# RWKV recurrence on one core: the state chain of a tile set among the doubling levels of the next tile, gate products in five blocks

## Chip, cores and metric

The kernel runs on one core of a Trainium2 chip. The metric is the device time of one launch, in microseconds (us), as the median over runs.

## What is computed

One step of a hybrid streaming encoder layer: a combined input projection of RMSNorm(h), chunked band attention for half of the heads, an RWKV-7 recurrence for the other half, gates, and an output projection. The change touches the recurrence. Per head it is

```
def step(S, inp):
    r_t, w_t, k_t, v_t, kk_t, a_t = inp
    sa = jnp.einsum('bhij,bhj->bhi', S, -kk_t)
    S = (S * w_t[:, :, None, :] + sa[..., None] * (kk_t * a_t)[:, :, None, :]
         + v_t[..., None] * k_t[:, :, None, :])
    y = jnp.einsum('bhij,bhj->bhi', S, r_t)
    return S, y
```

followed by a group norm of y, the bonus `sum(r * k * r_k) * v` and the gate silu(g). There are 2048 prompt frames (16 tiles of 128) and 8 running streams of 16 frames, which form a seventeenth tile with states of their own.

## The kernel before

Everything is in float32, or in two float32r parts for the wide products. The kernel has four phases: projection with attention, the shifted projections, `rwkv_phase` (recurrence, with the gate projection inside it), and the output projection.

In `rwkv_phase` a tile has two chunks of 64 frames and eight heads in four pairs, so eight units. A float32 product of 64x64 is recorded as two matmul entries, and the two halves of a unit run beside each other. For a tile t, in the order of its data:

- `mix`: LoRA products, sigmoids (`sig`, `a_gate` on ScalarE), the scan `acc` on VectorE, and the norm of the keys: `kk`, `kk_sq` on GpSimd, `kk_hi` on ScalarE, `kk_lo` on VectorE, and the `kk_sum` product on TensorE.
- `front`: `g_run`, `inv_g` (ScalarE, after a table load), `kk_n`, `ahat`, `rhat`, `bt`, `kt` (VectorE), `kmod`, `rkr`, `bmul` (GpSimd); the bonus products, the turns (`turn_two`), and the four Gram matrices B0, K0, B1, K1, masked by VectorE (L2123); then `a_eye` (GpSimd L1749), `z2`, `y2` (VectorE L2129, L2132) and the crossed copy (ScalarE L1910).
- levels (in `back`): the inverse of a triangular 64x64 matrix of each unit by doubling in five levels (three in the last tile). A level is the W products (L2401), the mask `w_mat` (VectorE L2145), the Q products (L2413), ScalarE's copy of the result (L1918, L1921) and VectorE's two transposes (L2150, L2153). W of the next level needs the copy, Q of the next level needs the transposes.
- chain (in `back`): for chunk 0 and then chunk 1: products of the state (L2422) into rhs, ScalarE's copy (L1930), `solve` (L2442), ScalarE's copy of u (L1934), products to the state (L2506), VectorE's add and decay (L2160, L2136), and `read_out` (L2451) into y.
- `tail`: `y_sum`, `y_centred`, `y_var` on VectorE, `y_sq` and the root on ScalarE, and on GpSimd `v_bonus` (L1784), then scale, gain, base and sum (L1787 to L1799).
- `gates`: 48 wide products (128x128 by 128x512) in two halves j of 24 for the gate projection, with splits of the input into two parts.

The order of each engine's queue is written by hand. Every run is a generator that yields a key ahead of each step, and `merged` always takes the step with the lowest key of the runs of a round; where keys are equal, the earlier run goes first. Engines meet by semaphores alone, so a key sets only an order. In round t the runs are `back(t)`, `tail(t-1)`, `front(t+1)`, `mix(t+2)` and `gates(t+1)`:

```
                run = [back(t, u, mode_of(t))]
                if t > 0:
                    run.append(tail(t - 1, 1 - u, "p"))
```

The levels stand at keys 4.1 l and 4.1 l + 2.1 for W and Q of level l, the chain at 20.5 and 26.85, the Grams at 25.05 and 28.15. Between W and Q, and between Q and W, stands a gate block (`GATE_BLOCKS`) of 4 or 5 products each: ten blocks a round, the last of 8. `free_bank` gives out two PSUM banks in turn in the order of `JOB_ORDER`; u is written into the level bank.

Of the kernel before, what the change touches and what calls it, by code (L numbers as in the profile page):

```python
# [22 lines left out]
P = 128  # L23
# [1213 lines left out]
def rwkv_phase(nc, io, shared):  # L1237

    with ExitStack() as ctx:
# [51 lines left out]
        bonus = sb2("bonus", [P, UNITS])  # L1291
# [42 lines left out]
        ps_u, ps_streams = ps_level[:, 0:512], ps_level[:, 512:1024]  # L1334
# [56 lines left out]
        def cols_of(n):  # L1391
# [8 lines left out]
        JOBS = ("decay", "iclr", "kk_sum", "k_tok", "b_tok", "B0", "B1", "K0", "K1", "bonus")  # L1400
# [9 lines left out]
        rhs_written, rhs_ready, u_written, u_ready = sem("rhs_written"), sem("rhs_ready"), sem("u_written"), sem("u_ready")  # L1410
# [5 lines left out]
        dec_keys = sem("dec_keys")  # L1416
# [3 lines left out]
        JOB_ORDER = ((("bonus", -1), ("decay", 0), ("k_tok", -1), ("B0", -1), ("B1", -1)),  # L1420
                     (("iclr", 0), ("b_tok", -1), ("K0", -1), ("K1", -1), ("kk_sum", 0)))
# [11 lines left out]
        def job_before(t, name):  # L1433
            b, i, off = place(name)
            r = t - off
            while r >= 0:
# [4 lines left out]
                if 0 <= r + o <= DEC:  # L1441
                    return n, r + o
            return None

        def free_bank(t, name):
# [4 lines left out]
            return ps_job[place(name)[0]], job_written[name]  # L1450

# [16 lines left out]
        def past(eng, t, *names):  # L1468

            for n in names:  # L1470
# [3 lines left out]
                       [(6, 12), (7, 13), (8, 22), (9, 26.1), (10, 28.4), (11, 28.5)])  # L1474
        GATE_BLOCKS = (((1.1, 5), (3.2, 5), (5.2, 5), (7.3, 5), (9.3, 4)), ((13.4, 4), (17.5, 4), (19.6, 4), (23.6, 4), (28.9, 8)))
        FIRST_SPLITS = (4, 5), (6, 7)
        GATE_W_AT = ((13, 14), (14, 15), (15, 18), (18.5, 23.5))
# [28 lines left out]
        def tiles(eng, front, back, mix=nothing, tail=nothing, gates=nothing, first_gates=nothing, out=nothing):  # L1506
# [44 lines left out]
        def _(sp):  # L1551
# [20 lines left out]
            def first_gates(t, u, mode):  # L1572
                if t == 1:
# [5 lines left out]
                    yield 30  # L1579
# [19 lines left out]
            def gates(t, u, mode):  # L1599
                if t == DEC:  # L1600
# [4 lines left out]
                    yield 11.8  # L1605
# [5 lines left out]
                for j in range(2):  # L1611
                    if t == DEC and j == 1:
                        yield 16
# [7 lines left out]
                        yield 30  # L1621
# [3 lines left out]
                    if j == 0 and t < DEC:  # L1625
# [3 lines left out]
                        yield 24.6  # L1629
                        sp.wait_ge(u_ready, 2 * t - 1)  # L1630
                    else:
                        yield (13.2, 33.5)[j]
# [20 lines left out]
            def mix(t, u, mode):  # L1653
# [7 lines left out]
                yield 24.7  # L1661
# [1364 lines left out]
```

## Time and profile before

| | us |
|---|---|
| median of 3 runs | 1640.91 (1640.88 to 1646.04) |
| the profiled execution | span 1640.3; no other time of it is recorded |
| TensorE busy | 1591.8 (97%) |
| VectorE, ScalarE, GpSimd busy | 806.8, 879.3, 498.8 |
| DMA | 184.4 MB, 112 GB/s on average |

Span is the time from the first to the last instruction. Busy TensorE counts an entry from its start to the end of its pipeline, so overlapping and waiting entries look alike, and starts say more than busy time. The recurrence phase lies between about 850 and 1440 us; a round begins with the W products of level 0.

### The profile page before, as it was taken

The numbers are of one execution on the slowest core, as the hardware profiler recorded it, in microseconds if no ns is written. First come the engines' busy times: TensorE is split into PE (matmuls) and PEld (weight loads), VectorE is DVE, ScalarE is ACT, GpSimd is POOL, SyncE is SP. The second block draws the span as 40 slices with busy tenths as digits, with TensorE's granted clock in tenths as the row PEclk, the third lists the DMA queues.
The fourth block names the chain that finished last, engine by engine and source line by source line (L and its number), as shares of the span: only waits on it lengthen the run. The fifth ranks groups of instructions, "written<-read, shape, count | busy, mean of one in ns | idle before, by whom it ended". The sixth has DMA issues, their size and how long they took to land. (4 is left out here: it accounts for less than half of the span.)

```text
span 1640.3 us, 46809 instructions
## 1 busy us (share of the span) xinstructions
PE 1591.8 (97%) x20218; PEld 1301.9 (79%) x20218; DVE 806.8 (49%) x1153; ACT 879.3 (54%) x1833; POOL 498.8 (30%) x354
## 2 busy tenths in 40 slices
PE   8999999999999899999998999999999997999999
PEld 7788888888888788899986777777777876777787
DVE  4344544454445531121226677667677677544432
ACT  6466566656665631222237777777777776224320
POOL 1423221222121012221223456455556456400000
PEclk9999999999999999999999999999999999999999
DMA  6323211122113543433353232232232236286652
GB/s 244 88 82 94 70 51 61 55 73 61 60 43 116 196 134 123 135 105 106 114 174 125 70 93 79 73 93 69 83 87 89 81 97 206 70 318 225 206 173 77
DMA packets 136302, 184.43 MB, mean 112 GB/s; under 512 B 59153, under 2 KB 88337, under 8 KB 135842
## 3 DMA queue, kind: packets, MB, share of 16 engines
q1 hardware_dynamic: 129186, 170.83, 32.3%
q10 hardware_dynamic: 6912, 10.62, 1.8%
q8 instruction: 160, 2.62, 0.7%
q14 instruction: 44, 0.36, 0.1%
HBM read 122.42 MB, written 59.55 MB: 111 GB/s over the span
## 5 line engine op out<-in xcount | busy, mean ns | idle before, releaser
L681 PE MATMUL a_ps_proj<-a_w_hi,a_x_hi 128*128 128x512 f32 x384 | 157.6, 410 | 2.5 <-ACT a_qk L431 1.4
L681 PE MATMUL a_ps_proj<-a_w_hi,a_x_lo 128*128 128x512 f32 x384 | 151.6, 395 | 0.0
L681 PE MATMUL a_ps_proj<-a_w_lo,a_x_hi 128*128 128x512 f32 x384 | 151.1, 393 | 0.0
L584 DVE SCALAR_TENSOR_TENSOR a_stage<-a_ps_s,a_new_bias 128x256 f32<-128x256 f32 x64 | 27.2, 425 | 241.5 <-PE a_ps_s L708 235.8
L2529 PE MATMUL r_ps_gate<-gate_w_hi,gate_x_hi 128*128 128x512 f32 x272 | 119.2, 438 | 5.2 <-PEq L66 3.4
L1187 DVE SCALAR_TENSOR_TENSOR j_out<-j_ps,j_rest,j_part 128x512 f32<-128x512 f32 (+2 forms) x45 | 29.0, 644 | 184.0 <-ACT j_last_cols L1131 139.1
L2529 PE MATMUL r_ps_gate<-gate_w_lo,gate_x_hi 128*128 128x512 f32 x272 | 111.6, 410 | 0.0
L360 POOL TENSOR_TENSOR a_xT<-a_xT,a_row 128x1024 f32<-128x1024 f32 x17 | 40.4, 2374 | 228.2 <-DMA a_row<-scratch_rstd 220.0
L469 ACT ACTIVATE a_stage<-a_stage,a_small 128x640 f32<-128x640 f32 (+4 forms) x128 | 95.8, 751 | 1.5 <-DVE a_small L592 1.5
L1061 POOL TENSOR_TENSOR j_v_prev<-j_v_prev,shift_x 128x512 f32<-128x512 f32 x17 | 22.2, 1307 | 228.3 <-DMA j_v_prev<-scratch_v_raw 216.7
L1129 ACT ACTIVATE j_part<-j_last_cols,j_shift_in 128x1 f32<-128x1 f32 x45 | 13.2, 294 | 141.7 <-PE j_ps L1220 141.7
L708 PEld LDWEIGHTS a_ps_s<-a_kT,a_qT 64*128 64x128 f32 x592 | 60.0, 186 | 33.5 <-issue 28.3
L681 PEld LDWEIGHTS a_ps_proj<-a_w_hi,a_x_lo 128*128 128x128 f32 x384 | 73.0, 190 | 16.5
L681 PEld LDWEIGHTS a_ps_proj<-a_w_hi,a_x_hi 128*128 128x128 f32 x384 | 73.1, 190 | 16.0 <-ACT a_qk L431 1.6
L592 DVE TENSOR_REDUCE a_small<-a_stage 128x2 f32<-128x1280 f32 (+4 forms) x64 | 84.5, 1320 | 2.2
L681 PEld LDWEIGHTS a_ps_proj<-a_w_lo,a_x_hi 128*128 128x128 f32 x384 | 73.4, 191 | 13.6
L478 ACT ACTIVATE a_stage<-a_ps_p 128x1024 f32<-128x1024 f32 (+3 forms) x60 | 56.5, 941 | 51.3 <-PE a_ps_s L730 51.2
L708 PE MATMUL a_ps_s<-a_kT,a_qT 64*128 64x128 f32 (+3 forms) x592 | 82.0, 390 | 1.0 <-ACT a_kT L460 0.8
L742 PE MATMUL a_ps_out<-a_stage,a_v 128*64 128x128 f32 x1120 | 75.3, 278 | 1.4 <-ACT a_stage L480 1.4
L2529 PE MATMUL r_ps_gate<-gate_w_hi,gate_x_lo 128*128 128x512 f32 x272 | 74.6, 406 | 0.0
L354 POOL TENSOR_TENSOR a_x_lo<-a_xT,a_x_hi 128x1024 fp32r<-128x1024 f32 x15 | 36.0, 2398 | 104.7 <-ACT a_x_hi L416 104.4
L742 PEld LDWEIGHTS a_ps_out<-a_stage,a_v 128*64 128x64 f32 x1120 | 59.8, 136 | 9.4 <-ACT a_stage L480 1.6
(414 smaller groups left out, 4677.6 us busy)
## 6 DMA issues: line engine op xcount, KB each, us to landing
a_xT<-in_x_T SPq DMA_DIRECT2D x17, 512.0 KB, 3.4
scratch_xT<-a_xT SPq DMA_DIRECT2D x17, 512.0 KB, 2.6
raw<-scratch_xT SPq DMA_DIRECT2D x17, 512.0 KB, 4.8
scratch_gates<-r_gate_out SPq DMA_DIRECT2D x34, 256.0 KB, 2.4
z_gate<-scratch_gates SPq DMA_DIRECT2D x17, 512.0 KB, 4.6
a_x<-in_x_prompt SPq DMA_DIRECT2D x16, 512.0 KB, 3.6
o_x<-in_x_prompt SPq DMA_DIRECT2D x14, 512.0 KB, 4.9
out_y_prompt<-o_y SPq DMA_DIRECT2D x14, 512.0 KB, 2.9
```

The lines of the kernel that those rows point to most:

```text
L354: nc.gpsimd.tensor_tensor(x_lo[n % 2][:], xT[n % 3][:], x_hi[n % 2][:].bitcast(F32), ALU.subtract).then_inc(x_lo_ready, 1)
L360: nc.gpsimd.tensor_tensor(xT[n % 3][:], xT[n % 3][:], by_token, ALU.mult).then_inc(x_by_row, 1)
L469: nc.scalar.activation(probs[s % 2][:, e, lo * P:WIN], probs[s % 2][:, e, lo * P:WIN], ACT.Exp, bias=neg_max[s % 2][:, e:e + 1], accum_out ...
L478: nc.scalar.activation(pT[:, :, lo:SLOTS - 1, :].rearrange("p e j n -> p e (j n)"), ps_p[:].rearrange("p (e n) -> p e n", e=2)[:, :, lo * ...
L584: nc.vector.scalar_tensor_tensor(out=out[:, :, OLD:WIN], in0=ps_new, scalar=SCALE, in1=new_bias[:, 2 * c:2 * c + 2, :], op0=ALU.mult, op1= ...
L592: nc.vector.tensor_reduce(neg_max[s % 2], out[:, :, lo * P:WIN], AX_X, ALU.max, negate=True).then_inc(max_ready, 1)
L681: mm = nc.tensor.matmul(ps_proj[:], a[n % 2][:, k, :], w[:, k, g * AW:(g + 1) * AW], start=(k == 0 and i == 0), stop=(k == KT - 1 and i == 2))
L708: return nc.tensor.matmul(out, qT[t % 2][half, c, :], kT[half, c, r:r + b - a, :].rearrange("p j n -> p (j n)"), start=True, stop=True)
L742: mm = nc.tensor.matmul(ps_out[e * HD:(e + 1) * HD, c * P:(c + 1) * P], v[:, ring(t, j), h * HD:(h + 1) * HD], pT[:, e, j, :], start=(j == ...
L1061: nc.gpsimd.tensor_tensor(v_prev[:], v_prev[:], v_raw[t % 2], ALU.subtract).then_inc(v_less, 1)
L1187: last = nc.vector.scalar_tensor_tensor(out=out[j][:, 0:n], in0=ps[j][:, 0:n], scalar=rest[:, b:b + 1], in1=part[j][:, 0:n], op0=ALU.mult, ...
L2529: mm = nc.tensor.matmul(ps_gate[:], x[:, k, :], w[:, j, k, :], start=i == 0, stop=i == 3 * KT - 1)
```

## The change

`back` is divided into `levels` and `chain`, and the chain of tile t-1 runs in round t, among the levels of tile t. The chain has its own keys on each engine, and its parts are in smaller groups. Both parts of the decay of the state stand behind their adds. u has banks of its own among the two job banks, `bonus` has three buffers instead of two. The 48 gate products come in five blocks. The last tile's chain follows in the same round. Many keys move with them.

```
-                     (("iclr", 0), ("b_tok", -1), ("K0", -1), ("K1", -1), ("kk_sum", 0)))
+        JOB_ORDER = ((("bonus", -1), ("k_tok", -1), ("B0", -1), ("B1", -1), ("decay", 0)),
+                     (("u0", -3), ("u1", -3), ("b_tok", -1), ("K0", -1), ("K1", -1), ("iclr", 0), ("kk_sum", 0)))
-        LEVEL_AT, CHAIN_AT = 4.1, (20.5, 26.85)
-        GRAM_AT = (25.05, 28.15)
+        LEVEL_AT, Q_AT, CHAIN_AT = 3.0, 1.4, (20.5, 26.85)
+        GRAM_AT = (13.6, 15.5)
-        GATE_BLOCKS = (((1.1, 5), (3.2, 5), (5.2, 5), (7.3, 5), (9.3, 4)), ((13.4, 4), (17.5, 4), (19.6, 4), (23.6, 4), (28.9, 8)))
+        GATE_BLOCKS = (((2, 8), (8, 8), (14.5, 8)), ((16.6, 10), (18.5, 14)))
...
-                run = [back(t, u, mode_of(t))]
+                run = [levels(t, u, mode_of(t))]
                 if t > 0:
-                    run.append(tail(t - 1, 1 - u, "p"))
+                    run += [chain(t - 1, 1 - u, "p"), tail(t - 1, 1 - u, "p")]
...
                 else:
-                    run.append(later(tail(DEC, 0, "s"), LAST_TAIL))
+                    run += [chain(DEC, u, "s"), later(tail(DEC, u, "s"), LAST_TAIL)]
```

TensorE's part of the new chain, and the steps around it (each line is a key and what is issued there):

```
+                yield 0.2
+                for c in range(PAIRS):
+                    value(t, u, 1, 0, c, ps_y, c == 0)
+                    last = from_state(0, 0, ps_rhs, c, False, c == PAIRS - 1)
+                yield 0.5
+                    from_key(0, c)
+                yield 1.6
+                    value(t, u, 1, 1, c, ps_y, False)
+                    last = solve(0, c)
+                yield 3.2
+                    from_state(0, 1, ps_y, c, False, False)
+                    value(t, u, 0, 1, c, ps_rhs, c == 0)
+                    last = to_state(0, c)
+                yield 3.5
+                read_out(0)
+                yield 6.2
+                    last = from_state(1, 0, ps_rhs, c, False, c == PAIRS - 1)
+                yield 6.5
+                    from_key(1, c)
+                    from_state(1, 1, ps_y, c, False, False)
+                yield 7.6
+                    first_values(t + 1, 1 - u, c)
+                    last = solve(1, c)
+                yield 9.2
+                    last = to_state(1, c)
+                yield 9.5
+                read_out(1).then_inc(ready["ps_y"], 1)
```

The other keys that the prediction speaks of, before and after:

| engine | step | before | after |
|---|---|---|---|
| TensorE | bonus; turns; LoRA; kk_sum | 11.5; 21.8; 15.5; 29 | 9.8; 10.6; 18; 26 |
| ScalarE | table load, g_run, inv_g; key norm | 1; 3.4 | 0.1; 2.3 |
| ScalarE | copies of Q | 4.1 l + 3.2 | 3 l + 1.9 |
| ScalarE | rhs, u of chunk 0; of chunk 1 | 21.2, 23.7; 27.55, 30 | 0.7, 2.2; 6.8, 8.2 |
| ScalarE | crossed z2; sig, a_gate; kk_hi; fac | 31.3; 16.6, 18.2; 21.7; 27.7 | 18.8; 19.3, 19.4; 21.7; 23 |
| ScalarE | copy of gate half 0; split; half 1 | 11.3; 26; 32.5 | 15; 25; 26.5 |
| VectorE | mask; transposes of level l | 4.1 l + 1.2; + 4 | 3 l + 0.6; + 2.4 |
| VectorE | add and decay of the state | 25.3; 31.7 and 14.7 | 3.7; 9.8 |
| VectorE | ahat; rhat; g_last | 6.3; 10.4; 17.8 | 10.3; 10.4; 10.5 |
| VectorE | y_sum, y_centred; y_var | 2; 7.7 | 12.2; 14.2 |
| VectorE | z2, y2; scan; kk_lo | 31.2, 31.4; 20.4; 23 | 18.4, 18.5; 21.5; 23 |
| GpSimd | kk; kk_sq | 13; 21.6 | 7; 18.75 |
| GpSimd | a_eye; v_bonus | 30.3; 8.8 | 17.4; 15.3 |
| GpSimd | scale; gain; base; sum of y | 18; 18.1; 18.2; 18.3 | 18.6; 18.65; 18.8; 18.9 |
| GpSimd | split of x | 33.7 | 26 |
| SyncE | r part of xs; v_tok | 24.7; 12 | 15; 18 |
| SyncE | gate stores; store of y | 24.6 and 33.5; 24.8 | 16 and 27; 26.5 |

## Rows read from the trace of the kernel before

**Rows 1.** Busy time in stretches; columns: stretch, length, five engines, clock, DMA share, GB/s.
```profile
887.40:917.90 30.50, 30.11 (x803) 23.95 (x804) 17.91 (x32) 21.52 (x47) 7.74 (x7) 1.00 0.21 64
917.90:1347.50 429.60, 421.57 (x11237) 335.14 (x11233) 303.84 (x491) 314.77 (x687) 233.66 (x183) 1.00 0.28 83
...
1382.60:1441.30 58.70, 50.94 (x745) 39.28 (x745) 35.63 (x45) 20.52 (x33) 26.17 (x15) 0.98 0.35 120
...
1256.40:1286.60 30.20, 30.00 (x807) 23.95 (x804) 21.56 (x36) 22.50 (x50) 16.74 (x14) 1.00 0.28 84
```

**Rows 2.** TensorE's timeline of one round and the next start: start, us, instruction, count.
```profile
1256.40 0.69 PE L2401 MATMUL r_ps_level<-r_y_mat,r_bm 64*64 64x64 f32 x32
...
1281.54 0.33 PE L2358 MATMUL r_ps_job<-r_late,r_bt 64*64 64x128 f32 x2
...
1282.43 0.25 PE L2442 MATMUL r_ps_level<-r_rhs,r_z_mat 64*64 64x64 f32 x2
...
1286.59 0.69 PE L2401 MATMUL r_ps_level<-r_late 64*64 64x64 f32 x32
1287.22 0.50 PE L2529 MATMUL r_ps_gate<-gate_w_hi,gate_x_hi 128*128 128x512 f32 x1
1287.56 0.39 PE L2529 MATMUL r_ps_gate<-gate_w_lo,gate_x_hi 128*128 128x512 f32 x1
...
1288.25 0.40 PE L2529 MATMUL r_ps_gate<-gate_w_hi,gate_x_hi 128*128 128x512 f32 x1
1288.58 0.27 PE L2413 MATMUL r_ps_level<-r_w_mat,r_late 64*64 64x64 f32 x2
```

**Rows 3.** VectorE's timeline of the same round.
```profile
1257.16 0.69 DVE L2145 TENSOR_TENSOR r_w_mat<-r_ps_level,consts 128x512 f32<-128x512 f32 x1 [0.67 <-PE r_ps_level L2401]
1257.76 0.68 DVE L2048 TENSOR_SCALAR r_kk_n<-r_ps_job 128x512 f32<-128x512 f32 x1
...
1260.65 0.45 DVE L2153 STREAM_TRANSPOSE r_z_cross<-r_y_cross 128x256 f32<-128x256 f32 x1 [0.43 <-ACT r_y_cross L1921]
...
1262.79 0.69 DVE L2082 TENSOR_TENSOR r_late<-r_kk_n,r_g_run 128x512 f32<-128x512 f32 x1
...
1265.72 1.47 DVE L2082 TENSOR_TENSOR r_late<-xs,r_g_run 128x512 f32<-128x512 f32 x1
...
1273.33 1.22 DVE L2070 TENSOR_TENSOR_SCAN r_acc<-consts,r_sig 128x512 f32<-128x512 f32 x1
...
1279.68 0.43 DVE L2136 TENSOR_TENSOR r_state<-r_state,r_g_last 128x256 f32<-128x256 f32 x1
```

**Rows 4.** ScalarE's timeline of the same round.
```profile
1256.54 1.28 ACT L1880 ACT_TABLE_LOAD   x1
1257.83 0.63 ACT L1887 ACTIVATE r_g_run<-r_acc 128x512 f32<-128x512 f32 x1
...
1259.14 0.60 ACT L1918 ACTIVATE r_y_mat<-r_ps_level 128x512 f32<-128x512 f32 x1 [0.16 <-PE r_ps_level L2413]
1259.78 0.84 ACT L1921 ACTIVATE r_y_cross<-r_y_mat 64x256 f32<-64x256 f32 x2
...
1271.71 1.15 ACT L1859 ACTIVATE r_sig<-r_ps_job,params 128x128 f32<-128x128 f32 x4
```

**Rows 5.** GpSimd's timeline around the same round.
```profile
1253.34 1.10 POOL L1749 TENSOR_TENSOR r_bm<-r_bm,consts 128x512 f32<-128x512 f32 x1 [7.70 <-DVE r_bm L2123]
...
1265.61 1.03 POOL L1716 TENSOR_TENSOR r_kk<-xs,params 128x512 f32<-128x512 f32 x1
1266.61 1.49 POOL L1787 TENSOR_TENSOR r_y_tok<-r_y_tok,r_small 128x512 f32<-128x512 f32 x1
```

**Rows 6.** Idle times of TensorE, in its timeline, and the stretch behind one of them.
```profile
887.43 0.69 PE L2401 MATMUL r_ps_level<-r_y_mat,r_bm 64*64 64x64 f32 x32 [1.72 <-ACT r_z_cross L1910]
...
1382.57 1.13 PE L2401 MATMUL r_ps_level<-r_y_mat,r_bm 64*64 64x64 f32 x32 [2.05 <-ACT r_late L1910]
...
1382.00:1386.00 4.00, 3.43 (x71) 3.01 (x72) 1.66 (x4) 2.72 (x5) 3.89 (x2) 0.57 0.19 68
```

More of the change, by code:

```diff
@@ L1290, in rwkv_phase @@
                   for i, n in ((1, "km"), (2, "bm")))
-        bonus = sb2("bonus", [P, UNITS])
+        bonus = [sb(f"bonus{i}", [P, UNITS]) for i in range(3)]
         z_mat, y_mat = ([sb(n, [P, UNITS, CH])[:], second(3, i, 2).rearrange("p (m l) -> p m l", m=UNITS)]
@@ L1504, in later, with tiles @@
                 yield key + by
-        def tiles(eng, front, back, mix=nothing, tail=nothing, gates=nothing, first_gates=nothing, out=nothing):
+        def tiles(eng, front, levels, chain=nothing, mix=nothing, tail=nothing, gates=nothing, first_gates=nothing, out=nothing):
             merged(mix(0, 0, "p"), first_gates(0, 0, "p"))
@@ L1694, in back @@
                                      states[:, :, now, :].rearrange("p c b d -> p c (b d)")).then_inc(stored, 16)
-            tiles(sp, front, back, mix, tail, gates, first_gates, out)
+            tiles(sp, front, nothing, chain, mix, tail, gates, first_gates, out)
             for j in range(2):
@@ L1826, in out @@
                     split_out_w(k)
-            tiles(pool, front, back, mix, tail, gates, out=out)
+            tiles(pool, front, nothing, chain, mix, tail, gates, out=out)
         @block.scalar
@@ L2037, in out @@
                     act.dma_start(rows_of(io["y_prompt"], D)[P:2 * P, OUT_X[j]], gate_out[j][:]).then_inc(y_stored[j], 16)
-            tiles(act, front, back, mix, tail, gates, first_gates, out)
+            tiles(act, front, levels, chain, mix, tail, gates, first_gates, out)
         @block.vector
@@ L2066, in mix @@
                     return
-                yield 20.4
+                yield 21.5
                 was_read(dve, t, "decay")
@@ L2137, in decay_state, with levels @@
                                         ALU.mult).then_inc(state_ready, 1)
-            def back(t, u, mode):
+            def levels(t, u, mode):
                 L = LEVELS[mode]
@@ L2284, in out @@
                 add_x(1, 0)
-            tiles(dve, front, back, mix, tail, gates, first_gates, out)
+            tiles(dve, front, levels, chain, mix, tail, gates, first_gates, out)
             add_x(1, 1)
@@ L2414, in back, with chain, from_key, from_state @@
                     last.then_inc(q_written, 1)
-                def from_state(n, kind, out, last_one):
-                    for c in range(PAIRS):
-                        if n == 0 and kind == 0:
-                            from_key(0, c)
-                        for g in range(2):
-                            last = nc.tensor.matmul(out[half(g), cols(n, c)], ar[u][half(g), c, n, kind, :], state[half(g), c, :],
-                                                    start=False, stop=last_one and c == PAIRS - 1)
+            def chain(t, u, mode):
+                L = LEVELS[mode]
+                def from_key(n, c):
+                    for g in range(2):
+                        nc.tensor.matmul(ps_s[half(g), cols(n, c)], k_swap[u][half(1 - g), unit(n, c), :], v_swap[u][half(1 - g), unit(n, c), :],
+                                         start=c == 0, stop=False)
+                def from_state(n, kind, out, c, start, stop):
+                    for g in range(2):
+                        last = nc.tensor.matmul(out[half(g), cols(n, c)], ar[u][half(g), c, n, kind, :], state[half(g), c, :],
+                                                start=start, stop=stop)
                     return last
@@ L2513, in back @@
+                        last.then_inc(done, 1)
+                        yield (26.2, 32.4)[n]
+                        was_read(pe, t, f"u{n}")
+                        last = read_out(n)
+                    last.then_inc(ready["ps_y"], 1)
                     yield 36.5
                     to_streams(1)
+                    return
+                yield 0.2
+                wait(pe, state_ready, 2 * t)
+                wait(pe, ready["y_centred"], t)
+                was_read(pe, t, "K1")
+                v_arrived(pe, t, u)
@@ new lines, in chain @@
+                for c in range(PAIRS):
+                    value(t, u, 1, 0, c, ps_y, c == 0)
+                    last = from_state(0, 0, ps_rhs, c, False, c == PAIRS - 1)
+                last.then_inc(rhs_written, 1)
+                yield 0.5
+                wait(pe, s_added, 2 * t)
+                was_read(pe, t, "k_tok")
+                for c in range(PAIRS):
+                    from_key(0, c)
+                yield 1.6
+                pe.wait_ge(rhs_ready, 2 * t + 1)
+                pe.wait_ge(z_ready, LP * t + L)
@@ L2600, in out @@
                     products(b // 12, b // 6 % 2, b % 6)
-            tiles(pe, front, back, mix, gates=gates, first_gates=first_gates, out=out)
+            tiles(pe, front, levels, chain, mix, gates=gates, first_gates=first_gates, out=out)
 def output_phase(nc, io, shared):
```

345 lines of the change are left out of this document (174 added, 171 removed).

## Prediction

> **What bounds the kernel now.** I read the stretches of the whole execution first [rows 1]. TensorE is busy nearly everywhere, so it sets the end, and the only thing to look for is what each microsecond of its order is spent on. The change touches the recurrence phase alone: a first round of 30.5 us, fourteen rounds of 429.6 / 14 = 30.7 us, one more, and the last with the output products. Busy time hides two things there, so I went to TensorE's timeline of one ordinary round, 1256.40 to 1286.59, 30.2 us [rows 2].
>
> The row of the first W product lasts 0.69 us for 32 entries (a float32 matmul of 64x64 is two entries), of which the last entry's own 0.22 us is pipeline: 0.47 us, 14.7 ns an entry. Gate products start 0.23 us apart (1287.56 to 1288.25 is three of them). By the code a round has 672 entries of 64x64 or narrower (9.9 us), 64 gram entries at 27.7 ns (their 1281.54 to 1282.43 is 0.89 us for 32: 1.8 us in all), 16 LoRA entries (0.9 us) and 50 wide products (11.7 us): 24.3 us. The rest is changes of shape and waits. A change of shape is seen around every gate block: the 32 W entries of 0.47 us take 0.63 us until the first gate product (1286.59 to 1287.22), and its five products of 0.23 take 1.36 us until the first Q product (1287.22 to 1288.58). That is 0.35 us a block, 3.5 us for ten blocks, and I allow 0.35 us for the LoRA block, whose 64x128 shape differs too. 24.3 + 3.5 + 0.35 = 28.1, so a round waits about 2.1 us now. The level chain itself waits hardly at all: the gate block between W and Q (1.35 us) covers the mask on VectorE, and the one after Q covers ScalarE's copy.
>
> **What the change takes away.** Five gate blocks a round instead of ten save 5 x 0.35 = 1.75 us. The products are the same 48, the recurrence's entries the same. The 2.1 us of waits now go as well, since the order that holds them is gone; that is the most that they can give. Together -3.85 us a round.
>
> **What it brings: waits.** The new keys put eight products between Q0 and W1 and between Q2 and W3, and none elsewhere in the levels. So each remaining step is covered only by chain products of the tile before, at 14.7 ns an entry. I walk the round in the order of the keys, engine by engine.
>
> W to Q: VectorE starts the mask 0.27 us after the last W entry, works 0.69 us [rows 3], and TensorE starts 0.05 us after it: 1.0 us. W0 is followed by 48 entries (0.7 us): 0.3 us of wait. W1 and W3 have 64 (0.94 us): 0.06 each.
>
> Round start: ScalarE does the gate copy, then the table load, g_run and inv_g (1.28 + 0.63 and about as much again [rows 4]) before the rhs copy; solve(0) stands 0.4 us.
>
> Q1 to W2: nothing lies between. ScalarE's copy is 0.60 us, with 0.26 before it and 0.05 behind: 0.95. Then Q2 needs z_cross: copy, the two halves of 0.84 us, the transpose of 0.45, then VectorE's mask behind it. That is 2.8 us from the last Q1 entry, against 0.95 + 0.47 + 0.70: 0.7 more.
>
> W4 to Q4: nothing lies between, and VectorE is late. Behind mask 3 its queue now has the state's add and decay, ahat, rhat, g_last, two transposes, y_sum and y_centred (key 12.2) before mask 4 (12.6). Instructions that need nothing of each other start 0.60 us apart at 0.69 us long (1257.16 to 1257.76), and the short ones (0.43 to 0.45) take 0.35 the same way [rows 3]; y_centred needs y_sum and starts after its end. 0.27 + 0.60 + 0.34 + 0.35 + 0.61 + 0.61 + 0.07 + 0.37 + 0.37 + 0.72 + 0.61 + 0.69 + 0.05 = 5.65 us from the last W3 entry to Q4, while TensorE has 0.47 + 0.47 + 0.5 + 0.94 + 0.47 = 2.9 us of work: 2.7 us of wait.
>
> Before kk_sum: this is the longest chain. From the last entry of the second gram: mask of B1 until 0.96; GpSimd adds the identity (1.10 us) until 2.1; z2, z_cross (0.84), then the sigmoids of the decay (1.15), which stand behind z_cross in ScalarE's queue, the scan (1.22), kk_sq on GpSimd (1.03, as kk, the same form), kk_lo (0.69, as ahat) [rows 3 to 5]. Back to back that is 8.0 us. But it will not be back to back. Rhat at 1265.72 lasts 1.47 us where its twin, ahat, lasts 0.69: GpSimd had begun an instruction at 1265.61 and ended it at 1266.64, and 0.14 before that end plus 0.69 is 1267.19, the end of rhat. An instruction with two SBUF inputs on VectorE waits for a GpSimd instruction that is under way. In the new order GpSimd takes y_scaled (1.49 us [rows 5]) in the moment a_eye ends, ahead of z2, and y_based (1.3 us by the nearest rows, the a_eye row's 1.10 and y_scaled's 1.49) as kk_sq ends, ahead of kk_lo. Each costs some 1.2 us: 10.3 us to kk_sum. TensorE has 10 products, LoRA and 14 products in the meantime, 2.6 + 1.05 + 3.5 = 7.1 us: 3.2 us of wait, 0.9 if the two collisions don't occur.
>
> The Trainium skill has the collision as a rule (GPSIMD Engine Reference, section Specifications): the SBUF interfaces of GpSimd are shared with VectorE, with contention for DVE instructions with two SBUF inputs. The trace agrees with it by the 1.47 us; leaving the collisions out would give 0.9 us for this wait and 15 x 2.3 = 34 us less in all.
>
> **The sum.** Waits: 0.3 + 0.4 + 0.95 + 0.7 + 0.1 + 2.7 + 3.2 = 8.35. A round: 30.2 - 3.85 + 8.35 = 34.7, +4.5 us; fifteen rounds (all but the first and the last) +67 us. In the first round the chain is missing (256 entries, -3.8 us) and the levels lose most of their cover, and the last takes those entries with the chain's copies between them, where TensorE idles now for 58.7 - 50.9 us [rows 1]; both together I put at +3 us, between -4 and +9. The DMAs move in SyncE's queue only: xs, gate_x and v_tok are issued earlier than needed by several us (and used a round later), so nothing; if one landed late, it would show as an idle kk or split of x. The third bonus buffer is free of cost, and so is u's new bank as long as VectorE has read kk_sum from it (0.68 us behind mask 0) before the rhs copy ends, which the walk gives; without that cover solve(0) stands up to 0.7 us more a round. 1640.3 + 67 + 3 = 1710. The span of 1640.3 us lies 0.6 us under the median of the runs, 1640.91, which gives 1711.
>
> **Unknown sizes.** The 2.1 us of present waits might stay in part (the mean round is 0.5 us longer than this one): from 0 to +0.5 a round. The collisions: from none to both. The ends of the first and last round: -4 to +9 us. So from 1711 - 34 = 1677 to 1711 + 8 + 6 = 1725 where the mechanism is the one above.
>
> **Rivals.**
> (a) *The clock falls in the new waits.* It is at full rate (2.4 GHz) in the fourteen rounds [rows 1], whose waits are short. But after the idle 2.05 us before 1382.57 the stretch 1382 to 1386 has 0.57 granted, so some us at 1.2 GHz [rows 6]. The new order has 2.7 and 3.2 us of idle in each round. A stretch of 4 us at 0.57 costs 4 x 0.43 = 1.7 us where TensorE sets the pace. If one falls in every round: 1711 + 15 x 1.7 = 1737, more with two. Against it: the idle 1.72 us before 887.43 left the first round at 1.00. The Trainium skill (TensorE: Matmul & The Clock Gate, What's actually happening) says that the throttled state is the default and that activity releases it, which speaks for this rival.
> (b) *One of the two long waits isn't there*, because queues shift against each other: 1711 less 15 x 2.7 = 1671.
> (c) *Faster: the waits are covered.* The place is VectorE's queue between mask 3 and mask 4, and the z2 to kk_lo chain under the 14 products; if both keep up, waits fall to 2.45 us, a round takes 28.8, and the time is 1711 - 15 x 5.9 = 1623. It decides below 3.85 us of waits a round. For it: the key positions of kk_sum (26) and the gram (15.5) leave that chain much room, and VectorE is busy only 21.6 of 30.2 us. Against it: the queues are in order and each of the two sums needs nothing but durations of rows.
> (d) *It does nothing*, since savings and waits cancel: waits of exactly that size, 1641.
>
> **How the numbers follow.** The forecast (waits as walked, 1677 to 1725) 0.58, (a) 0.22, (b) 0.10, (c) 0.07, (d) 0.03. The range from 1668 to 1748 leaves out (c), (d) and the far end of (a). Faster by over 0.3%, about what a measurement can tell from no change: 0.07; within: 0.02; slower: 0.91.
>
> **What would show it.** In the profile after: five gate blocks a round; first W products some 34.7 us apart; Q4 waiting for the mask (VectorE, w_mat) by 2 to 3 us each round, kk_sum's product for kk_lo by 3 us; W2 idle 0.9 us before it, by ScalarE's copy; z2 and kk_lo longer than 1.3 us in many rounds, where ahat, of the same form, takes 0.69. VectorE's instructions between mask 3 and mask 4 in the order given. I am wrong if rounds are under 31 us, or if the waits sit at the rhs and u copies of the chain, which I take as covered by the gate blocks; wrong in size if the granted clock of the rounds is under 0.95.

## The result and the profile after

The changed kernel takes 1763.82 us (median of 4 runs, 1758.67 to 1770.5) where the kernel before, run beside it, takes 1643.47: a ratio of 1.074, 95% interval 1.0706 to 1.0773 (ratios here and below are to the kernel before, run in the same batch; the two medians by themselves give 1.073). The prediction named the side and nearly all the waits; its 1711 us and its upper end, 1748, are too low.

The stretches, to be held against [rows 1]: the first round, the fourteen rounds behind it, and 4 us behind one of the long waits.

```profile
885.40:920.80 35.40, 29.60 (x560) 23.11 (x556) 16.58 (x28) 17.66 (x40) 6.00 (x6) 0.81 0.07 24
920.80:1464.80 544.00, 437.84 (x11229) 362.94 (x11228) 302.52 (x491) 313.26 (x689) 227.41 (x182) 0.94 0.22 65
997.30:1001.30 4.00, 4.00 (x132) 3.69 (x134) 1.29 (x2) 2.70 (x5) 4.00 (x4) 0.57 0.30 62
```

A round lasts 544 / 14 = 38.9 us against 30.7: +8.2, where +4.5 was forecast. In the profiled executions (spans 1640.3 and 1768.7) the fourteen rounds bring 114 us of the 128, the first round 5, and the rest comes behind them. The profiled execution of the changed kernel is the longest of its four, 7 us over their median, so what is read from it is a little high. The granted clock of the fourteen rounds is 0.94, not 1.00: 65 us of them are at 1.2 GHz, in 19 stretches. The prediction had a clock under 0.95 as its sign of a wrong size. The third row is such a place, some microseconds at 1.2 GHz directly behind a wait for `kk_sum`.

TensorE's waits in the same fourteen rounds (total us, times, longest):

```profile
PE r_ps_job L2329 <- DVE r_kk_lo L2079: 42.7, 14, 3.1
PE r_ps_level L2403 <- DVE r_w_mat L2151: 30.1, 22, 2.5
PE r_ps_level L2391 <- ACT r_late L1918: 5.1, 7, 0.7
PE r_ps_level L2391 <- ACT r_y_mat L1918: 5.1, 7, 0.7
PE r_ps_level L2391 <- issue: 4.0, 5, 1.8
PE r_ps_level L2403 <- issue: 4.0, 3, 1.7
PE r_ps_y L2418 <- issue: 3.7, 2, 2.5
PE r_ps_rhs L2418 <- issue: 2.5, 1, 2.5
PE r_ps_s L2412 <- issue: 2.4, 2, 1.4
PE r_ps_rhs L2335 <- issue: 1.8, 2, 0.9
```

The first four rows are the waits that the prediction walked: `kk_sum` for `kk_lo`, Q of level 4 for its mask (27.5 of the 30.1 us; the rest is Q of level 2), W of level 2 for ScalarE's copy. The rows with "issue" are idle time whose end the profile puts down to no engine and no DMA, called time with no releaser below. They sum to 21.7 us (with the shorter rows left out here) where the kernel before has 4.4 us, and the prediction had nothing on them.

One round's end, VectorE and then GpSimd, to be held against [rows 3] and [rows 5]:

```profile
1177.34 0.65 DVE L2202 TENSOR_REDUCE r_small<-r_ps_y 128x8 f32<-128x512 f32 x1
1178.03 0.69 DVE L2205 SCALAR_TENSOR_TENSOR r_y_tok<-r_small,r_ps_y 128x512 f32<-128x512 f32 x1
1178.63 0.68 DVE L2151 TENSOR_TENSOR r_w_mat<-r_ps_level,consts 128x512 f32<-128x512 f32 x1
...
1186.04 1.52 DVE L2135 TENSOR_TENSOR r_z_mat<-r_bm,consts 128x512 f32<-128x512 f32 x1 [0.70 <-POOL r_bm L1751]
...
1192.13 1.68 DVE L2079 TENSOR_TENSOR r_kk_lo<-r_sig,r_kk_hi 128x512 fp32r<-128x512 f32 x1 [1.26 <-POOL r_sig L1729]
```

```profile
1185.96 1.05 POOL L1789 TENSOR_TENSOR r_y_tok<-r_y_tok,r_small 128x512 f32<-128x512 f32 x1
...
1192.00 1.27 POOL L1798 TENSOR_TENSOR r_y_tok<-r_y_tok,params 128x512 f32<-128x512 f32 x1
```

Mask 4 stands behind `y_sum` and `y_centred`, as walked. `z2` and `kk_lo` start just after a GpSimd instruction did and last 1.52 and 1.68 us (the first experiment has both at 0.69). Their ends, 1187.56 and 1193.81, are 0.55 and 0.54 us behind the ends of the two GpSimd instructions, as with the row of 1.47 us in [rows 3]. And TensorE in that round:

```profile
1179.37 0.27 PE L2403 MATMUL r_ps_level<-r_late,r_w_mat 64*64 64x64 f32 x2 [2.47 <-DVE r_w_mat L2151]
...
1194.07 0.47 PE L2329 MATMUL r_ps_job<-r_kk_hi,r_head_sums 128*128 128x512 f32 x1 [3.07 <-DVE r_kk_lo L2079]
```

With the pipeline's 0.2 us these are 2.7 and 3.3 us; forecast were 2.7 and 3.2.

### The profile page after: what moved, and what is told of

Read it like the earlier page. It is cut to its first block and busy times, and to the rows that moved or that the text cites. A ratio compares the mean times of both kernels' runs of the same rounds, so it can differ in the third digit from the quotient of the medians.

```text
span 1768.7 us, 46844 instructions
## 1 busy us (share of the span) xinstructions
PE 1611.2 (91%) x20218; PEld 1334.8 (75%) x20218; DVE 798.1 (45%) x1153; ACT 876.7 (50%) x1833; POOL 488.1 (28%) x354
## 3 DMA queue, kind: packets, MB, share of 16 engines
q1 hardware_dynamic: 129186, 170.83, 30.1%
## 5 line engine op out<-in xcount | busy, mean ns | idle before, releaser
L2151 DVE TENSOR_TENSOR r_w_mat<-r_ps_level,consts 128x512 f32<-128x512 f32 x83 | 56.7, 683 | 77.0 <-PE r_ps_level L2391 77.0
L681 PEld LDWEIGHTS a_ps_proj<-a_w_hi,a_x_hi 128*128 128x128 f32 x384 | 72.6, 189 | 14.7 <-ACT a_qk L431 1.6
L2583 PEld LDWEIGHTS r_ps_gate<-gate_w_hi,gate_x_hi 128*128 128x128 f32 x272 | 53.8, 198 | 22.5 <-issue 8.1
```

Of the source, the lines that this page charges most:

```text
L681: mm = nc.tensor.matmul(ps_proj[:], a[n % 2][:, k, :], w[:, k, g * AW:(g + 1) * AW], start=(k == 0 and i == 0), stop=(k == KT - 1 and i == 2))
L2151: nc.vector.tensor_tensor(w_mat.rearrange("p (n m) l -> p n m l", n=NCH), ps_w.rearrange("p n (m l) -> p n m l", m=PAIRS), level.rearrange ...
L2583: mm = nc.tensor.matmul(ps_gate[:], x[:, k, :], w[:, j, k, :], start=i == 0, stop=i == 3 * KT - 1)
```

## The experiments

Three causes were held against each other: the waits as walked (theory A in most expectations), the clock, and, once the rows with "issue" had been seen, the supply of instructions to TensorE. The share of each wait was tested by taking the wait away.

**GpSimd's steps of y apart from z2 and kk_lo.** The keys of scale, gain, base and sum (the steps between them are left out):

```
-                yield 18.6
-                yield 18.65
-                yield 18.8
-                yield 18.9
+                yield 17.2
+                yield 17.3
+                yield 26.2
+                yield 26.3
```

> The changed kernel with GpSimd's y_scaled and y_gained moved ahead of a_eye, and y_based and the last sum behind the split of x, so that GpSimd starts nothing of its own as z2 or kk_lo becomes ready. Theory A (collisions of VectorE with GpSimd, as walked): z2 and kk_lo take 0.7 us again in place of 1.5 to 1.7, TensorE's wait before kk_sum falls from 3.0 us to about 0.9, and 14 or 15 rounds give 2.1 us each, some 30 us: 1734. Theory B (the wait before kk_sum is bounded by something else, or what it gives comes back in the next round, whose rhs and key norm start earlier behind the same ScalarE queue): z2 and kk_lo are short, but the time stays within 8 us of 1764. Theory C (TensorE's clock is what long idle times cost): more than 30 us, since stretches at the lower clock go as well.

Measured 1738.18 us, ratio 1.0598 (1.0566 to 1.0629), 0.014 less than the changed kernel: 23 us. Its VectorE groups in the fourteen rounds, and TensorE's waits:

```profile
L2079 DVE TENSOR_TENSOR r_kk_lo<-r_sig,r_kk_hi 128x512 fp32r<-128x512 f32 x14 | 9.7, 692 | 18.4 <-POOL r_sig L1729 18.4
L2135 DVE TENSOR_TENSOR r_z_mat<-r_bm,consts 128x512 f32<-128x512 f32 x7 | 4.8, 693 | 4.9 <-POOL r_bm L1751 4.9
```

```profile
PE r_ps_job L2329 <- DVE r_kk_lo L2079: 18.1, 14, 1.6
PE r_ps_y L2335 <- ACT r_rhs L1932: 14.3, 14, 1.1
```

```profile
918.30:1425.70 507.40, 421.02 (x11233) 346.40 (x11232) 278.60 (x491) 310.62 (x688) 217.87 (x181) 0.98 0.23 70
```

Both instructions are back at 0.69 us (they averaged 1.63 and 1.52), and the wait falls from 42.7 to 18.1 us. Theory A; but a part comes back, a wait for the rhs copy at solve of chunk 0, 14.3 us where it was 1.1, since the round now starts before ScalarE is through its table load, `g_run` and `inv_g` (the run with the rhs copy first, below, bears this out). The clock came along: 20 us of the fourteen rounds are at 1.2 GHz in place of 65, and no fall begins right behind W0, where seven did. So the gain is not that of the wait alone.

**VectorE's y_sum and y_centred behind mask 4.**

```
-                yield 12.2 if mode == "p" else 2
+                yield 12.65 if mode == "p" else 2
```

> The changed kernel with VectorE's y_sum and y_centred behind the mask of level 4 (key 12.65 in place of 12.2). Theory A (VectorE's queue between mask 3 and mask 4 sets Q of level 4): the wait before that Q falls by the 0.61 + 0.72 us that the two take in the queue, from some 2.3 us to 1.0, 15 rounds give 20 us: 1744. Theory B: the two instructions move into the chain from the Gram masks to kk_sum or delay the square of y and so GpSimd's scale of y, and the wait appears before kk_sum instead: within 6 us of 1764.

Measured 1745.52, ratio 1.0646 (1.0606 to 1.0685): 0.0094 less, 15 us. The waits for masks are 14.9 us in place of 30.1, the one for `kk_lo` stays at 42.2, and 4.4 us of new waits stand at the Grams. Theory A, with 15 of its 20 us.

**Both edits.**

> The changed kernel with both earlier edits: GpSimd's four steps of y away from z2 and kk_lo, and VectorE's y_sum and y_centred behind mask 4. Theory A (the two waits are independent terms of the round): the ratios to the kernel before add, 1.0740 less 0.0142 less 0.0094 = 1.050, some 1723. Theory B (the ends of the two waits lie on one chain, from mask 4 over the Grams to kk_sum, so that one saving includes the other): 1.058 to 1.060. Clock: with both long waits shortened to about 1.2 us, at most three stretches at the lower clock are left in the fourteen rounds.

Measured 1733.25, ratio 1.0541 (1.0513 to 1.057): five sixths of the sum of both. It lies halfway between A's 1.050 and B's 1.058, and the interval leaves out both, so the two waits are in the main separate terms, not quite. 27 us are left at the lower clock in seven stretches, where at most three were expected.

**The wait for kk_lo filled with work.** Twelve products of 128x128 by 128x512 ahead of `kk_sum`:

```
+                ps, done = free_bank(t, "kk_sum")
+                if 2 < t < DEC:
+                    for i in range(12):
+                        nc.tensor.matmul(ps[:], head_sums[:], w_hi[:, 0, 0, :], start=True, stop=True)
                 need(pe, t, "kk_hi", "kk_lo")
```

> The changed kernel with 12 more products of 128x128 by 128x512 ahead of kk_sum in thirteen rounds, in the wait for kk_lo, into the bank of kk_sum, which kk_sum then overwrites. At 0.23 us each they are 2.8 us of work where TensorE idles 3.0 us. Theory A (the fall of the clock is brought about by that idle time): granted clock stays up behind it, the time falls by 5 to 20 us in spite of the added work. Theory B (the clock falls for other reasons, such as the small products at a row, or the wait alone costs): no change within 6 us, the clock's low stretches stay as many. Theory C (the wait is in truth shorter than the profile shows, or the products hold up something): slower, up to 13 x 2.8 = 36 us.

Measured 1763.82, ratio 1.0758 (1.0728 to 1.0787), no change in time, as theory B had it. The wait is gone and the time is the same with some 36 us of work added, so it was a true wait:

```profile
PE r_ps_level L2406 <- DVE r_w_mat L2151: 33.2, 21, 2.5
PE r_ps_level L2394 <- issue: 8.0, 6, 2.6
PE r_ps_job L2332 <- DVE r_kk_lo L2079: 5.5, 14, 2.9
```

In the changed kernel seven of the nineteen stretches at the lower clock begin within 1 us behind W0 of a round, right behind this wait; here none does. But others begin 10 to 14 and 21 to 25 us into a round, and in all 48 us are at the lower clock in place of 65 (11 stretches in place of 19, where B had as many as before). Work in one idle time keeps the clock up there and not in the rest of the round.

**The kernel before with the bonus products by themselves.**

```
-                    if t > 0:
-                        value(t - 1, 1 - u, 1, n, c, ps_y)
                 last.then_inc(done, 1)
+                if t > 0:
+                    for n, c in all_units:
+                        value(t - 1, 1 - u, 1, n, c, ps_y)
```

> The kernel before with one thing of the change in it: the bonus products come first, all 32 entries, and the 32 of the values of y behind them, instead of the two kinds in turn. The same work in the same place. Theory P (small products of 64x64 run at 14.7 ns an entry only where products that stay in their half of the array alternate with products that cross it, and at 27 to 29 ns where one kind follows itself): the 64 entries take 1.8 us in place of 0.94, 15 rounds of 0.85 us, 1641 to 1654. Theory Q (an entry costs 14.7 ns whatever its neighbours): within 3 us of 1641.

Measured 1652.51, ratio 1.0074 (1.0047 to 1.0101), 12 us: theory P. TensorE's timeline of one place:

```profile
1272.71 0.87 PE L2343 MATMUL r_ps_job<-params,r_rk 64*64 64x2 f32 x26
...
1273.57 0.80 PE L2331 MATMUL r_ps_y<-r_v_swap,r_km 64*64 64x64 f32 x21
```

Less the last entry's own 0.19 and 0.22 us these are 27 and 29 ns an entry, where the 64 entries in turn took 0.91 us, 14.2 ns each. The whole is 0.6 us longer, and VectorE's mask then comes late for one Q by another 0.57 us a round.

**The gate products in five blocks, in the kernel before.** The other half of the change without the first:

```
-        GATE_BLOCKS = (((1.1, 5), (3.2, 5), (5.2, 5), (7.3, 5), (9.3, 4)), ((13.4, 4), (17.5, 4), (19.6, 4), (23.6, 4), (28.9, 8)))
+        GATE_BLOCKS = (((3.2, 8), (7.3, 8), (9.3, 8)), ((17.5, 10), (23.6, 14)))
```

> The kernel before with its gate products in five blocks of 8, 8, 8, 10 and 14, at keys 3.2, 7.3, 9.3, 17.5 and 23.6, and nothing else: the other half of the change, without the chain moved. Theory A: five changes of shape saved, -1.75 us a round; but W0 to Q0, W1 to Q1 and W3 to Q3 have nothing between them (1.0 us of wait each), the chain from the last Gram to z2 has lost its 8 products (1.84 us), and rhs and u of the chain one block each, some 0.5 us: +3.5 us a round, 1641 + 53 = 1694. Theory B (the changes of shape are what a round loses, the waits overlap): within 10 us of 1641.

Measured 1732.61, ratio 1.0548 (1.0508 to 1.0589): theory A, and some 37 us more than it said.

```profile
PE r_ps_level L2413 <- DVE r_w_mat L2145: 39.9, 42, 1.2
PE r_ps_level L2401 <- ACT r_z_cross L1910: 26.6, 15, 2.1
PE r_ps_job L2325 <- DVE r_late L2123: 7.0, 7, 1.0
PE r_ps_job L2325 <- DVE r_km L2123: 6.8, 7, 1.0
```

42 waits are the three bare masks of fourteen rounds, 0.95 us each, as said; the last two rows are `kk_sum` waiting for a Gram's mask, by the order of the banks the one that frees its bank. The expectation did not have this, nor the 37 us at the lower clock. The blocks' 0.35 us are worth far less than what the blocks cover.

**Ten blocks in the changed kernel.**

```
-        GATE_BLOCKS = (((2, 8), (8, 8), (14.5, 8)), ((16.6, 10), (18.5, 14)))
+        GATE_BLOCKS = (((1.2, 5), (2.5, 5), (4.2, 5), (5.5, 5), (7.2, 4)), ((8.6, 4), (10.1, 4), (11.5, 4), (13.0, 4), (18.5, 8)))
...
-                yield 15
+                yield 7.9
                 copy_gates(t, 0)
```

> The changed kernel with its 48 gate products in ten blocks as before (5, 5, 5, 5, 4, 4, 4, 4, 4, 8), one between every W and Q and between every Q and W, the last 8 ahead of kk_sum; ScalarE's copy of the first half comes at 7.9. Theory A (the walk: waits are what is not covered): the waits in the levels, 0.3 + 0.95 + 0.7 + 0.1 + 2.7 us, fall by 3.3 us, but only 8 products stand between the second Gram and kk_sum where 24 stood, so that wait grows by 16 x 0.23 = 3.7 us, and five more changes of shape cost 1.75: 2.1 us a round more, some 30 us slower than the changed kernel, 1795. Theory F (instruction supply: TensorE starves in long rows of small products): the idle time that nothing releases falls from 1.6 us a round to the 0.45 of before, and the low stretches of the clock are fewer: within 10 us of 1764 or faster.

Measured 1824.92, ratio 1.11 (1.1075 to 1.1124), slower than theory A said.

```profile
PE r_ps_job L2329 <- DVE r_kk_lo L2079: 68.4, 14, 5.4
PE r_ps_gate L2583 <- ACT r_gate_out L1963: 22.4, 14, 1.6
PE r_ps_job L2359 <- DVE r_km L2129: 10.3, 7, 1.5
...
PE r_ps_y L2446 <- issue: 2.1, 2, 1.8
```

The waits in the levels are gone, the one for `kk_lo` has grown, and 1.6 us a round at the copy of the first gate half and 2.9 at the Gram masks are new; the copy is of this edit's own making. But the time with no releaser fell from 21.7 to 2.1 us: of theory F this much holds, and no more. The time at the lower clock, which F had falling, rose from 65 to 100 us; thirteen of the seventeen stretches begin in or right behind the wait for `kk_lo`, now up to 5.4 us long.

**Seven blocks**, on top of both edits, with shorter rows of small products:

```
-        GATE_BLOCKS = (((2, 8), (8, 8), (14.5, 8)), ...
+        GATE_BLOCKS = (((2, 4), (5.5, 4), (8, 4), (13, 4), (14.5, 8)), ...
```

> The changed kernel with GpSimd's y steps and VectorE's y sums moved as in the run of both (ratio 1.054), and its first gate half in 4, 4, 4, 4 and 8 products at keys 2, 5.5, 8, 13 and 14.5 in place of 8, 8 and 8, so that a block stands between Q1 and W2 and between W4 and Q4, and no row of small products is longer than some 190 entries where it was up to 270. Theory A (waits alone): 0.74 us at W2 and 0.88 us at Q4 go, two changes of shape come (0.7 us): -0.9 us a round. Theory F (long rows starve TensorE of instructions, and waits bring the low clock): idle time with no releaser falls from 18 us in the fourteen rounds to under 8, worth 0.6 us a round more, and low clock from 27 us to under 14, 0.4 us more: -1.9 us a round in all, ratio 1.037. Under 1.04 speaks for F, 1.045 or more for A alone.

Measured 1719.23, ratio 1.046 (1.0429 to 1.0491). The waits for the copy and the mask are gone, as A says, but F's rows grew where F had them fall:

```profile
PE r_ps_level L2391 <- issue: 10.2, 6, 2.8
PE r_ps_y L2446 <- issue: 5.7, 3, 2.5
PE r_ps_level L2403 <- issue: 3.9, 6, 1.4
PE r_ps_job L2346 <- issue: 3.6, 3, 1.6
```

In all 29.7 us with no releaser, where the run of both edits has 20.4, and 44 us at the lower clock in place of 27, where F had under 14. So the length of a row of small products alone is not what decides. A new theory: their density over several microseconds, since taking out a wait made the stretch denser.

**The same 256 small entries in one row, or in four**, in the kernel before (W of level 4 nine times, or W of levels 0 to 3 three times; the output is the same):

```
-                    for c in range(PAIRS):
+                    for c in list(range(PAIRS)) * (9 if l == 4 and 0 < t < DEC - 1 else 1):
```

> The kernel before with the 32 entries of W of level 4 given nine times over in fourteen rounds, all in one row: 256 more entries, same output. Their own time at 14.7 ns is 3.8 us a round. Theory S (instructions of TensorE come in packets of 16 KB, about 128 entries of small products each, that never start less than 3.3 us apart, so 26 to 28 ns an entry is all that can be kept up once the store is used): the row lasts some 2 to 3 us longer than its 288 x 14.7 ns, idle time with no releaser appears in nearly every round, +5.8 to +6.8 us a round, ratio 1.049 to 1.058. Theory E (an entry costs its 14.7 ns and stalls in the changed kernel have another cause): +3.8 us a round, ratio 1.032.

> The same 256 more entries a round, but as two more repeats of W in each of the levels 0 to 3, with gate blocks between them. Theory S: a round of 34.5 us has time for nine or ten packets, 1032 entries need eight, and no row is longer than 96 + 64 entries more than before: the supply nearly keeps up, idle time with no releaser under 0.8 us a round, +3.8 to +4.6 us a round, ratio 1.032 to 1.039. Theory E: 1.032, as the run before; it and the run before are then the same within 0.004.

One row: 1736.79, ratio 1.0593 (1.0573 to 1.0612). Four rows: 1719.55, ratio 1.0477 (1.0455 to 1.0499). Both are over the 1.032 of theory E, and they differ by 17 us with the same work. This excludes E; theory S has the one row nearly right and the four rows too short (it had 1.032 to 1.039). TensorE's timeline in one row of the first, with the entries between two stops:

```profile
1042.75 2.09 PE L2401 MATMUL r_ps_level<-r_y_mat,r_bm 64*64 64x64 f32 x128 [0.73 <-issue]
1046.22 1.51 PE L2401 MATMUL r_ps_level<-r_y_mat,r_bm 64*64 64x64 f32 x89 [1.38 <-issue]
```

128 entries run at (2.09 - 0.22) / 127 = 14.7 ns, then the engine stands 1.38 us: 3.47 us for 128, 27 ns an entry. The DMA records have packets of 16 KB on the instruction queue that start never less than 3.2 us apart in the recurrence phase of any run here, one for some 128 entries. The two stops shown end 2.4 us after such a packet started, and in the changed kernel the stop of 2.52 us that ended at 1130.06 had one 2.3 us before its end. This holds throughout: of the changed kernel's 21 stops with no releaser in the fourteen rounds 20 end 2.2 to 2.9 us behind the start of a packet, and of its 51 waits for an engine 2, where 11% of the time lies so. So these stops are waits for instructions. What keeps the packets 3.2 us apart no run shows. Four rows cost 5.4 us a round and not the 3.8 to 4.6 expected: they too leave 1.7 us a round with no releaser. In both runs the clock stays at 1.00 in the fourteen rounds: the one row has 37 us of such stops, none over 1.9 us, and no fall.

**kk_sum in the next round**, behind W0 and the rhs products, on top of both edits (`sum_keys` holds the two products):

```
+            def front(t, u, mode):
+                if t > 1:
+                    yield 0.35
+                    sum_keys(t)
```

> As the run before, and the kk_sum products of a tile in the next round, behind W of level 0 and the rhs products of the chain, where nothing reads their result before. Theory A (what is left of the wait for kk_lo, 1.2 us a round, is a matter of the queue's order): the 0.47 us of W0 and 0.5 us of rhs products stand in it, the wait falls to 0.3 us; a change of shape is added (0.35 us); the round is 0.5 us shorter, 8 us in all, 1.045. Theory B: kk_sum's reader on VectorE and the key norm on ScalarE come later by as much, and the wait comes back at solve(0) or at the bonus: the same as the run before, or up to 10 us slower.

Measured 1738.38, ratio 1.0582 (1.0542 to 1.0623), 7 us over the run before by the ratios: theory B. The wait for `kk_lo` has fallen from 20.0 to 3 us, and that for the rhs copy has grown from 12.8 to this:

```profile
PE r_ps_y L2339 <- ACT r_rhs L1932: 29.1, 14, 2.1
```

**The rhs copy first on ScalarE**, on top of the seven blocks:

```
-                    yield (0.7, 6.8)[n] if mode == "p" else CHAIN_AT[n] + 0.7
+                    yield (0.05, 6.8)[n] if mode == "p" else CHAIN_AT[n] + 0.7
```

> As the run before, and ScalarE's copy of the rhs of chunk 0 ahead of its table load, g_run and inv_g. Theory A (solve of chunk 0 waits for that copy by nothing but ScalarE's queue): the wait, 0.9 us a round, falls to 0.4 or less, 0.5 to 0.9 us a round, ratio 0.005 to 0.008 lower than the run before. Theory B (g_run and inv_g, now 1 us later, are what kt, bt and the turns wait for): no gain, and the wait is at the turns or at W1.

Measured 1722.54, ratio 1.0482 (1.045 to 1.0515): that wait, 13.6 us, is gone, and 5.7 us for the copy of u and 6.0 for W of level 2 took its place. No gain, as B said, but by other waits than it named.

**Nine blocks in the kernel before**, key 19.6 joined to 17.5, and the same with ten for the last tile:

```
-        ... ((13.4, 4), (17.5, 4), (19.6, 4), (23.6, 4), (28.9, 8)))
+        ... ((13.4, 4), (17.5, 8), (23.6, 4), (28.9, 8)))
```

> The kernel before with the four gate products of key 19.6 joined to those of key 17.5, nine blocks in place of ten. Behind Q of level 4 stand 96 entries of key and state products and 64 of the turns before solve needs ScalarE's copy, 2 us of cover. Theory A (a change of shape costs 0.35 us where its cover isn't needed): -0.35 us a round, 5 us, ratio 0.997. Theory F (the row of small products grows from some 150 entries to over 200): idle time with no releaser grows from 4 us to 12 us or more in the fourteen rounds, and takes the gain back or more: 0.999 to 1.006.

> The kernel before with nine gate blocks as in the earlier run, but ten where the products of the last tile's gates are made, as in that run the last full round took 40.8 us where before it took 35.1, which took back the 0.31 us of each of the fourteen others. Theory A: the last round is as before, 14 x 0.31 = 4.3 us faster, ratio 0.9975, which five rounds can just tell. Theory B (the end is set by the z2 chain against the last output loads and not by the blocks, the rounds' gain is absorbed there): 1.000.

Ratios 1.0 (0.998 to 1.0019) and 0.9991 (0.9975 to 1.0007): 0.997 lies outside the first interval, 0.9975 at the very end of the second. The stretches of the first: fourteen rounds, and the last full one.

```profile
912.30:1337.70 425.40, 416.49 (x11242) 335.38 (x11237) 303.47 (x491) 315.34 (x688) 233.91 (x184) 1.00 0.28 84
1337.70:1378.40 40.70, 32.55 (x787) 25.94 (x785) 28.70 (x39) 21.94 (x39) 23.84 (x14) 0.86 0.48 163
```

The rounds are 0.3 us shorter, 425.4 against 429.6 us, so a change of shape is worth about its 0.35 us where its cover isn't needed. Theory F's idle time did not come: 6.2 us with no releaser, not 12. The last full round takes 40.7 and 39.8 us in the two profiles, where it was 35.1, with a clock of 0.86 and 0.91. Ten blocks there did not mend it, and in the run with one long row, which leaves this round as it was, it takes 41.1 us in the profile at a clock of 0.92. So the blocks need not be the cause, and there is one profile a kernel; why it grows was not found. No version of these beats the kernel before by more than the measurement can tell.

## Why the prediction was right and wrong

Over the fourteen rounds of fifteen profiles (before, after, and thirteen of the runs above, all but the last) I fitted the length of a round as one constant a kernel, plus a price for each microsecond at the lower clock and for each with no releaser. The prices come out at 0.32 and 1.02 us, with 0.4 us left over a round. The price of the clock is an average: fitted one kernel at a time it lies between 0.14 (ten blocks, where 23 of some 100 us at the lower clock are TensorE's waits) and 0.55, and the changed kernel's own rounds give 0.53 (standard error 0.11) and 0.6 for time with no releaser. By the prices of all the 8.2 us are:

| | before | after | difference |
|---|---|---|---|
| round without either | 30.35 | 35.80 | +5.45 |
| lower clock, 0 and 4.6 us a round | 0 | 1.5 | +1.5 |
| no releaser, 0.33 and 1.54 us a round | 0.3 | 1.6 | +1.2 |

By the changed kernel's own prices the clock would have 2.4 us and the missing releaser 1.0, so each of the two is known to within some 1 us.

**Right.** Slower, by waits between the levels and before `kk_sum`; each of the three long ones where it was put. The collisions were the boldest step, and the first run shows them. The longest terms, 2.7 and 3.2 us, came out at 2.7 (where nothing stopped TensorE before it) and 3.3. W of level 2 waits 0.73 us, 0.95 with the pipeline's share, as walked.

**Wrong: "the 2.1 us of waits now go as well".** This was no wait, and all of it stays. The remainder of the sum was called so because all 672 small entries were priced at the 14.7 ns of a W row. By the code a W row alternates products that stay in their half of the array with such that cross it; where one kind stands alone an entry takes 27 to 29 ns. By the code 96 entries of the kernel before stand alone, 96 x 14 ns = 1.3 us of work that stays. For the other 0.8 us no run shows what it is, only that it is no wait for an engine: those are 0.05 us a round in the trace of before, and all its idle time 0.57. The changed kernel has 128 lone entries, 0.5 us more, of which the lone bonus is measured above.

Against it some waits were walked too long. With the pipeline's share they last, on average over the fourteen rounds: before `kk_sum` 3.25 us (forecast 3.2), W of level 2 0.9 (0.95), Q of level 4 2.2 (2.7), as stops ahead of it eat into it, Q of level 2 0.3 (0.7; it is 0.5 in eight rounds and nothing in six), Q of level 0 nothing (0.3), Q of levels 1 and 3 nothing (0.1), solve of chunk 0 0.1 (0.4). That is 6.75 in place of 8.35. So 34.7 + 2.1 + 0.5 - 1.6, and 0.2 because a mean round of before is 30.35 by the fit and not 30.2, is 35.9; the constant of the fit is 35.8.

**Wrong: nothing for the supply of instructions.** The same 736 entries of levels, chain, turns and Grams stand in the first 26 of 37 us in the new order; most gate products and the long wait have the rest. Before, ten blocks spread them out. This is 1.2 us a round. That the stops are waits for instructions is shown by the packets, and that they grow with density by the one row against four; that they cost just this much rests on the fit.

**Rival (a) as an alternative.** It was given 0.22 as another case, at 1.7 us a round. It came together with the forecast, at some 1.5 us (up to 2.4): the two are not exclusive, and the waits of the forecast were its condition. The filled wait shows the condition: no fall behind it where there had been seven. The Trainium skill (TensorE: Matmul & The Clock Gate, What's actually happening) has the throttled state as the default that activity releases. The trace agrees: none of the fourteen rounds of before, with 0.57 us of idle time each, has a fall, and those of the changed kernel, with 7.6 us each, have 19. The price is from the fit alone; no run held the clock and changed nothing else.

In numbers, the round came out 3.7 us longer than the forecast's +4.5: 2.1 and 0.5 for the work taken for waits, 1.2 for the supply, 1.5 for the clock, less 1.6 of waits. Clock and shortened waits nearly cancel.

**The ends.** Outside the fourteen rounds the profiles have 14 us more, where 7.5 were forecast: the first round 5, the last round with all behind it 12.5, the round behind the fourteen 1.5 less, and the time ahead of the first round 2 less.

**The parts of the change.** Five blocks alone cost 0.055, ten blocks with the moved chain 0.110 (of which the new wait for the gate copy, 1.6 us a round, is some 0.014), both together 0.074. The reading that fits is that the moved chain fills some of the gaps that the missing blocks leave, and that with ten blocks in place it only takes cover from the end of the round; no run tests it by itself. After all repairs that were tried the changed order stands at 1.046.

## What to carry to other kernels

What is left when the known work is taken from a round is not yet a wait: look in the idle column whether it is there before it is given back to the change. A block between two dependent steps is cover first and a change of shape second; here it covered about 1 us and cost 0.35. Filling an idle time with small products can move the bound to the supply of their instructions, so wide and small products want to be mixed over the whole round. And a long wait can cost more than its length, by the clock behind it.

## What the runs showed of the hardware

- Entries of 64x64 in float32 took 14.7 ns each where products that stay in their half of the array alternate with such that cross it, 27 to 29 ns where one kind follows itself.
- In a long row TensorE ran 128 entries at 14.7 ns and then stopped for 1.38 us, 27 ns an entry over both. Packets of 16 KB on the instruction queue started at least 3.2 us apart, and 20 of 21 stops in the changed kernel ended 2.2 to 2.9 us behind the start of one.
- A block of 128x128 products among 64x64 ones cost 0.35 us by the timeline and 0.3 us a round by the run with nine blocks for ten.
- A VectorE instruction with two SBUF inputs that starts just behind a GpSimd instruction took 1.52 to 1.68 us in place of 0.69; it ended 0.55 us behind the GpSimd instruction.
- A microsecond at 1.2 GHz cost about a third of a microsecond here by the fit over all profiles, 0.14 to 0.55 by kernel; half the clock alone would make it a half. A part of the difference is seen: a W row wholly inside such a stretch takes 26.5 ns an entry (15 of 16 such rows of the run with ten blocks) against 15 outside, so it does not take twice the time. In the changed kernel TensorE idles 0.2 of the 65 us, so waits inside these stretches are not the reason there; the rest is open.
- Stops of up to 1.9 us, 37 us of them in 521, brought no fall of the clock in the run with one long row. In the run with five blocks in the kernel before nine falls begin 0.8 to 2.4 us into a round, behind a wait of 1.7 to 2.1 us for the crossed copy.
